# A hybrid decoder layer: x loaded features first, its norm factor applied in ACT's evacuations, the sample tile reordered, and a buffer of its own for the closing down-projection weights

## What is computed

```python
hn = rmsnorm(x, norm1_g)                   # x * rsqrt(mean(x*x) + eps) * g
proj = hn @ w_in                           # 1024 -> 3608 columns
# ... two head groups: gated linear attention (GLA), gated delta rule (GDN) with a short conv
x = x + mix @ w_out                        # 1024 -> 1024
hn2 = rmsnorm(x, norm2_g)
up = causal_dwconv(hn2 @ w_up, ...)        # 1024 -> 2 * 2816, width 3
x = x + (silu(a_f) * b_f) @ w_down         # 2816 -> 1024
y = rmsnorm(x, norm_f_g)
```

## Time and profile before

| what | value |
|---|---|
| median of three runs (lowest, highest) | 3583.7 us (3581.7, 3585.63) |
| the profiled execution's own time | 3583.03 us |
| its span, first to last instruction | 3581.2 us |
| mean granted TensorE clock | 0.984 |
| PE busy | 3482.3 us, 97% of the span |
| DVE, ACT, POOL busy | 58%, 24%, 16% |
| DMA | 225 MB, 63 GB/s over the span |
| mixer, start to barrier | 0 to about 1865 us |
| pass 0 and pass 1 of the MLP | from about 1866 us and from about 2683 us |

### The profile page before, as it was taken

One profiled execution on the slowest core, in us unless ns is written; L12 is line 12 of the kernel. 1 busy time (PEld: TensorE's weight loads), 2 busy tenths in 40 slices (PEclk: granted clock), 3 DMA queues, 4 the chain that ended last, 5 costly groups with the idle time before them and its releaser, 6 DMA issues. The chain is left out here.

```text
span 3581.2 us, 48600 instructions
## 1 busy us (share of the span) xinstructions
PE 3482.3 (97%) x16521; PEld 2439.3 (68%) x16521; DVE 2086.7 (58%) x4762; ACT 873.4 (24%) x1864; POOL 587.8 (16%) x921
## 2 busy tenths in 40 slices
PE   7999999999999999999789999999999999999997
PEld 4666666666666666666557777777758788778774
DVE  2456555545656554456335666656686666666666
ACT  2222322222233223222202212121223222222223
POOL 1111001111111011111143111111133211211110
PEclk9999999999999999999879999999999999999998
DMA  5022212111221211122541111111133111111101
GB/s 203 10 62 70 70 59 70 51 49 53 70 70 59 70 58 48 47 65 65 163 129 53 47 48 40 42 35 59 36 90 134 45 36 36 47 47 36 44 27 71
DMA packets 207293, 225.00 MB, mean 63 GB/s; under 512 B 12908, under 2 KB 151700, under 8 KB 207203
## 3 DMA queue, kind: packets, MB, share of 16 engines
q1 hardware_dynamic: 207203, 223.90, 20.2%
HBM read 194.19 MB, written 29.67 MB: 63 GB/s over the span
## 5 line engine op out<-in xcount | busy, mean ns | idle before, releaser
L613 PE MATMUL mixer_bank<-arena,hnt 128*128 128x451 f32 x2176 | 920.2, 552 | 2.2 <-DVE hnt L1213 1.5
L1837 PE MATMUL mlp_bank<-arena,ws 128*128 128x176 f32 (+1 forms) x3520 | 658.1, 340 | 10.9 <-ACT raw L2017 7.5
L1837 PEld LDWEIGHTS mlp_bank<-arena,ws 128*128 128x128 f32 x3520 | 589.4, 191 | 49.0 <-ACT raw L2017 9.2
L613 PEld LDWEIGHTS mixer_bank<-arena,hnt 128*128 128x128 f32 x2176 | 387.6, 191 | 296.4 <-issue 289.2
L1909 PE MATMUL mlp_bank<-arena 128*128 128x512 f32 x1120 | 493.7, 592 | 0.0
L2279 DVE TENSOR_TENSOR acc<-acc,mlp_bank 128x512 f32<-128x512 f32 x560 | 370.6, 685 | 57.1 <-PE mlp_bank L1909 54.5
L1909 PEld LDWEIGHTS mlp_bank<-arena 128*128 128x128 f32 x1120 | 211.5, 190 | 231.3 <-issue 205.7
L550 POOL TENSOR_TENSOR ex<-dtt,level 128x512 f32<-128x512 f32 (+1 forms) x114 | 143.1, 1255 | 1089.9 <-DVE dtt L1435 727.2
L2246 DVE SCALAR_TENSOR_TENSOR mcv<-raw,cf,mcv 128x512 f32<-128x512 f32 (+2 forms) x440 | 286.2, 667 | 60.9 <-ACT mcv L1990 50.5
L629 PE MATMUL mixer_bank<-wo,th 128*128 128x512 f32 (+1 forms) x544 | 265.5, 613 | 4.4 <-DMA wo<-in_w_out_dram 4.4
L1837 PE MATMUL mlp_bank<-arena 128*128 128x176 f32 (+1 forms) x1320 | 254.3, 343 | 10.9 <-POOL ident_mlp L2153 10.1
(11 more groups left out here) (323 smaller groups left out, 4176.2 us busy)
## 6 DMA issues: line engine op xcount, KB each, us to landing
wo<-in_w_out_dram SPq DMA_DIRECT2D x272, 256.0 KB, 2.8
arena<-in_w_up_dram SPq DMA_DIRECT2D x44, 512.0 KB, 5.1
wu<-in_w_up_dram SPq DMA_DIRECT2D x44, 512.0 KB, 5.1
arena<-in_w_down_dram SPq DMA_DIRECT2D x44, 512.0 KB, 4.2
arena<-in_w_in_dram SPq DMA_DIRECT2D x8, 1804.0 KB, 17.0
xt<-in_x_prompt_dram SPq DMA_DIRECT2D x16, 512.0 KB, 3.5
xr<-in_x_prompt_dram SPq DMA_DIRECT2D x16, 512.0 KB, 3.6
resid<-yo SPq DMA_DIRECT2D x16, 512.0 KB, 3.4
```

The costliest lines, as they stand in the source:

```text
L613: x = pe.matmul(bank[ring(g)][0:N, 0:GW], hnt[:, k, 0:N], w[:, k, g * GW:(g + 1) * GW], start=(k == 0), stop=(k == KT - 1))
L1837: x = pe.matmul(out[:, 0:N], left[:, k, :], xb[:, slot, k, g * N:(g + 1) * N], start=first and k == 0, stop=k == HK - 1, skip_group_check= ...
```

## The change

x is also given to the kernel features first, as `x_t`. The front of a tile loads both: `xt` for the sum of squares only, and `xc` (new, 128 x 8 x 128) with features on partitions. DVE multiplies `xc` by the gain straight into `hnt`; the multiplication by the factor and the eight turns are gone, and the factor is applied by ACT as the scale of its eight evacuations per tile, now ACTIVATE with a scale for each partition. Since `x_rs` must live until those are done, its last step moves behind the eighth.

In the sample tile the tanh and the norm sums use `th_s`, which lies in `xc`; DVE's second evacuation of the output projection stands behind the first predicated copies; all state loads stand behind the last slice of `w_out`; `keep_y` and the wait for the states stand behind the masked copies of q; the masked copies of k are made by ACT in place of POOL.

In the MLP the closing weights go into `wd_last`, which lies in the up-weights' buffer `wu[1]` and is loaded when the last up-product of the pass is done; loads at the boundary are reordered around it, and POOL makes only the first group of input sums at once and the others when the combinations are through.

```diff
+        xc = sb("xc", [C, KT, C])
+        th_s = xc[:, :, :].rearrange("p k i -> p (k i)")[:, 0:CT * S].rearrange("p (c i) -> p c i", c=CT)
...
         def _(sp):
+            x_columns = x_t.rearrange("(k p) n -> p k n", p=C)
+            sp.dma_start(xc[:, :, :], x_columns[:, :, 0:C]).then_inc(s_xc_loaded, 16)
             sp.dma_start(xt[:, :], x_prompt[0:C, :]).then_inc(s_x_loaded, 16)
...
             with sp.Fori(1, TILES - 2) as t:
                 before = sp.snap(t - 1)
-                sp.wait_ge(s_hn_turned, t + 2)
-                sp.dma_start(xt[:, :], x_prompt[bass.ds(t * C + 2 * C, C), :]).then_inc(s_x_loaded, 16)
+                rows = bass.ds(t * C + 2 * C, C)
+                sp.wait_ge(s_x_squared, t + 2)
+                sp.dma_start(xt[:, :], x_prompt[rows, :]).then_inc(s_x_loaded, 16)
+                sp.wait_ge(s_hn_out, t + 2)
+                sp.sem_inc(s_held, 1)
+                sp.dma_start(xc[:, :, :], x_columns[:, :, rows]).then_inc(s_xc_loaded, 16)
...
             for i in range(4, 20):
-                if i == 8:
-                    sp.wait_ge(s_hs_cleared, 1)
-                if 8 <= i < 12:
-                    sp.dma_start(hs_gla[rows_of[i - 8], i - 8, :, :], state_gla[i - 8]).then_inc(s_st_loaded, 16)
                 sp.wait_ge(s_wo_used, 16 * (t - 1) + i - 3)
                 wo_chunk(t - 1, i)
+            sp.wait_ge(s_hs_cleared, 1)
+            for h in range(H):
+                sp.dma_start(hs_gla[rows_of[h], h, :, :], state_gla[h]).then_inc(s_st_loaded, 16)
...
# gpsimd: the two loops of masked copies of k (L564 to L574) go; before the early input sums:
+            gp.wait_ge(s_masked_w, 1)
...
# tensor: front_turn is gone everywhere; the sample's norm sums read th_s
...
# scalar, evacuate
                 act.wait_ge(s_proj_done, GROUPS * (m - 1) + g + 1)
-                act.copy(proj[0:N, g * GW:(g + 1) * GW], bank[ring(g)][0:N, 0:GW]).then_inc(s_proj_out, 1)
+                act.wait_ge(s_x_rsed, m)
+                act.activation(proj[0:N, g * GW:(g + 1) * GW], bank[ring(g)][0:N, 0:GW], ACT.Identity,
+                               scale=x_rs[0:N, :]).then_inc(s_proj_out, 1)
...
# scalar, mixer
-                if out:
+                if out and not sample:
                     act.wait_ge(s_wo_used, 16 * t)
-                act.activation(th[:, :, 0:N], cv[:, :, 0:N], ACT.Tanh, scale=0.5).then_inc(s_conv_tanh, 1)
+                tq = th_s if sample else th
+                act.activation(tq[:, :, 0:N], cv[:, :, 0:N], ACT.Tanh, scale=0.5).then_inc(s_conv_tanh, 1)
...
                 fill(2)
+                if sample:
+                    act.wait_ge(s_proj_done, GROUPS * n)
+                    act.wait_ge(s_ked_out, n)
+                    for b in range(NB):
+                        x = act.activation(mk_gla[b], ked[0:S, :], ACT.Identity, scale=rows_s[:, b:b + 1])
+                    x.then_inc(s_masked_k, 1)
+                    act.wait_ge(s_kh_made, n)
+                    act.wait_ge(s_conv_stored, 16 * (NB + 1))
+                    for b in range(NB):
+                        x = act.activation(mk_gdn[b], kh[0:S, :, :], ACT.Identity, scale=rows_s[:, b:b + 1])
+                    x.then_inc(s_masked_k, 1)
...
                 inverse_rms(1, None)
                 fill(7)
+                front(2)
...
# vector
-            def front_norm(m, N):
-                dve.wait_ge(s_x_rsed, m)
-                dve.tensor_scalar(xt[0:N, :], xt[0:N, :], x_rs[0:N, :], None, ALU.mult)\
-                    .then_inc(s_x_normed, 1)
             def front_out(m, N):
-                dve.wait_ge(s_hn_turned, m)
+                dve.wait_ge(s_xc_loaded, 16 * m)
                 dve.wait_ge(s_proj_done, GROUPS * (m - 1))
-                for b in range(2):
-                    x = dve.tensor_tensor(hnt[:, 4 * b:4 * b + 4, 0:N], heads(b)[:, :, 0:N],
-                                          g1[:, 4 * b:4 * b + 4].unsqueeze(2).to_broadcast([C, 4, N]), ALU.mult)
-                x.then_inc(s_hn_out, 1)
+                dve.tensor_tensor(hnt[:, :, 0:N], xc[:, :, 0:N], g1[:, :].unsqueeze(2).to_broadcast([C, KT, N]),
+                                  ALU.mult).then_inc(s_hn_out, 1)
...
-                turn_levels(0 if sample else 6, NL + 1)
+                if sample:
+                    turn_levels(0, len(levels))
+                    evacuate_out(t, 1, C)
+                turn_levels(len(levels) if sample else 6, NL + 1)
...
                 if sample:
-                    dve.wait_ge(s_st_loaded, 16 * 2 * H)
                     dve.wait_ge(s_qg_made, n)
...
                     x.then_inc(s_masked_qk, 1)
+                    keep_y(t, C)
...
# mlp
+        wd_last = [wu[1][:, i, :, :].rearrange("p k n -> p (k n)") for i in range(2)]
...
             def loop(ps):
...
-                down(ps, PAIRS - 1)
+                if ps == 0:
+                    up(1, 0, 0)
+                sp.wait_ge(s_m3, group(ps, FT, 0))
+                for p in range(2):
+                    r0 = (2 * PAIRS - 2 + p) * C
+                    sp.dma_start(wd_last[p], w_down[r0:r0 + C, :]).then_inc(s_last_loaded, 16)
+
+            def scale(ps):
+                sp.wait_ge(s_down_done, first_out(ps, PAIRS - 1))
                 sp.dma_start(gf, norm_f_g.partition_broadcast(C).rearrange("p (e d) -> p e d", e=2))\
...
             loop(0)
-            up(1, 0, 0)
             x_blocks(1)
+            scale(0)
+            sp.wait_ge(s_down_done, Q0[1])
             up(1, 1, 1)
...
             loop(1)
+            scale(1)
...
             def close(ps):
-                pe.wait_ge(s_wd_loaded, 32 * PAIRS * (ps + 1))
+                pe.wait_ge(s_last_loaded, 32 * (ps + 1))
...
             def x_sums(ps):
+                gp.wait_ge(s_act_made, J0[ps])
                 for g in range(G):
+                    if g == 1:
+                        gp.wait_ge(s_combined, 21 * ps)
```

More of the change, by code:

```diff
@@ L405, in _ @@
                 wo_chunk(0, i)
[L406 to L409, removed]
+            for m in (2, 3):
+                rows = slice(m * C - C, m * C)
+                sp.wait_ge(s_x_squared, m - 1)
+                sp.dma_start(xt[:, :], x_prompt[rows, :]).then_inc(s_x_loaded, 16)
+                sp.wait_ge(s_hn_out, m - 1)
+                sp.dma_start(xc[:, :, :], x_columns[:, :, rows]).then_inc(s_xc_loaded, 16)
             with sp.Fori(1, TILES - 2) as t:
                 before = sp.snap(t - 1)
-                sp.wait_ge(s_hn_turned, t + 2)
-                sp.dma_start(xt[:, :], x_prompt[bass.ds(t * C + 2 * C, C), :]).then_inc(s_x_loaded, 16)
+                rows = bass.ds(t * C + 2 * C, C)
+                sp.wait_ge(s_x_squared, t + 2)
+                sp.dma_start(xt[:, :], x_prompt[rows, :]).then_inc(s_x_loaded, 16)
+                sp.wait_ge(s_hn_out, t + 2)
+                sp.sem_inc(s_held, 1)
+                sp.dma_start(xc[:, :, :], x_columns[:, :, rows]).then_inc(s_xc_loaded, 16)
                 wo_chunks(before, 20)
@@ L587, in _ @@
         def _(pe):
[L588 to L595, removed]
             def project(m, part, N):
@@ L985, in front_norm @@
                     act.wait_ge(s_x_lned, m)
+                    act.wait_ge(s_proj_out, GROUPS * (m - 1))
                     act.activation(x_rs[0:N, :], x_ln[0:N, :], ACT.Exp, scale=-0.5).then_inc(s_x_rsed, 1)
@@ L1097, in mixer @@
                 for p in range(2):
-                    x = act.activation(th[:, 4 * p:4 * p + 4, 0:N], heads(3 + p)[:, :, 0:N], ACT.Ln,
+                    x = act.activation(tq[:, 4 * p:4 * p + 4, 0:N], heads(3 + p)[:, :, 0:N], ACT.Ln,
                                        bias=eps4[:, :])
@@ L1103, in mixer @@
                 act.wait_ge(s_norm_ln, n)
-                act.activation(th[:, 0:4, 0:N], th[:, 0:4, 0:N], ACT.Exp, scale=-0.5, bias=lnq[:, :])
-                act.activation(th[:, 4:8, 0:N], th[:, 4:8, 0:N], ACT.Exp, scale=-0.5)\
+                act.activation(tq[:, 0:4, 0:N], tq[:, 0:4, 0:N], ACT.Exp, scale=-0.5, bias=lnq[:, :])
+                act.activation(tq[:, 4:8, 0:N], tq[:, 4:8, 0:N], ACT.Exp, scale=-0.5)\
                     .then_inc(s_norm_rs, 1)
@@ L1440, in mixer @@
                     .then_inc(s_ab_made, 1)
-                if out and sample:
-                    keep_y(t, C)
                 dve.wait_ge(s_egrow_made, n)
@@ L1912, in down, with plain @@
                         bank_free(ps, i, 28 + e)
-                        plain(bank[4 + e], 2 * p, 8, e, S)
-            def plain(out, a, t, e, N):
+                        plain(bank[4 + e], 2 * p, wd, 8, e, S)
+            def plain(out, a, right, t, e, N):
                 for j in range(2):
-                    x = pe.matmul(out[0:N, :], act_[a + j][:, t * C:t * C + N], wd[j][:, e * 512:e * 512 + 512],
+                    x = pe.matmul(out[0:N, :], act_[a + j][:, t * C:t * C + N], right[j][:, e * 512:e * 512 + 512],
                                   start=(j == 0), stop=(j == 1))
@@ L2411 @@
```

(3 more changed lines are left out.)

68 lines of the change are left out of this document (26 added, 42 removed).

## The result

The changed kernel takes 3552.2 us (median of four runs, 3550.79 to 3554.07) against 3584.28 for the kernel before, measured beside it; the ratio is 0.9914, with a 95% interval of 0.9902 to 0.9926. The forecast was 3550.5. The medians lie 32.1 us apart, where 32.5 were forecast. The profiled execution has a span of 3550.5 us, 30.7 less than before, and a granted clock of 0.988 instead of 0.984. PE's busy time fell by 28.0 us, to 3454.3, and ACT's rose to 25% of the span.

A forecast was written before the change was run, and what follows sets the result against it. PE, busy 99.7 of 100 us in the loop, was taken as the bound, with gains where it stands still: -3.4 + 0 - 9.5 - 12 - 7.6 = -32.5, taking 3583.03 to 3550.5 us; range 3539 to 3563.

The forecast's parts named there:

- The loop: Fifteen loop tiles: a wait for ACT's copy replaces the eight removed turns; change 0, ends +1 and -15.4 us.
- rival (a): Loop: the removed turns are worth their time, 15 x 1.03 us more gain, 3535 us; chance 0.06.
- Rival (b): Loop: the clock falls at the new wait, 1.7 us lost per tile, 26 in all, 3576 us; chance 0.08.
- Rival (c): Loop: the clock falls and stays low, 6.9 us per tile, 103 in all, 3653 us, slower; chance 0.04.
- The start: Ahead of tile 0's turns: ACT's copies begin 4.6 us earlier, less the new load; -3.4 us (-4.6 to -1.6).
- the 1.2 us taken off for the new load: Start: the 512 KB xc load costs 1.9 us less 0.7 of slack; bounds nothing and 3 us.
- The sample tile: Sample tile: L747 starts at 1764.3 instead of 1774.2, 9.9 us less; taken as -9.5, bounds 11.4 and 5.
- three edits act in series: Sample tile: GLA loads behind slices, tanh waiting only for taps, keep_y behind masked copies; then states are late; 9.5 us.
- The pass boundary: Between MLP passes: earlier closing-weight load removes a 5.11 us stall and close ends at 2671; -12 us (-5 to -13).
- they can cost a us that the earlier start of ACT there gives back: Pass 1, first groups: deferred input sums lie beside them, costing a us that ACT's earlier start offsets.
- Rival (d): Pass boundary: POOL and DVE still collide, half the gain there, 3556 us; chance 0.14.
- The end: Last close: the 5.98 us stall and the low clock behind it both go; -7.6 us, bounds -5 and -9.

## Why the prediction was right

**The loop** was the main decision, and it came out as argued: not the 15 x 1.03 of rival (a), but a wait of 0.87 in the place of turns of 1.03, the tile at 103.65 us as before (stretch +0.10). ACT's scaled evacuations took 0.64 us each where the copies took 0.53, the 0.1 that I gave them, and in the loop no wait of PE names them. Rival (b) did not come at 0.87 between the wide turns of the loop, but its mechanism is there: at 1.84 it takes 18 us, and ahead of the sample tile's narrow turns 0.87 is enough (with 0.17 in its place the clock stayed at 1.00). Rival (c), I wrote, decides from 2.2 us per tile on; the longer wait cost 2.2 per tile on average, wait and clock together, and just that brought the kernel level with the one before. A fall that stays for 14 us was not seen in the loop.

**The start** gave 5.03 where I had 3.4, and more than its bound of 4.6. The mis-sized step is the 1.2 us taken off for the new load. Its price was right (1.8 for another one; the 2304 KB of its working should be 2316, which changes nothing), and the 0.4 less for rows of 512 bytes, which rests on no number given there, did not show: another such load cost the full 1.8. The first product is 0.97 later:

```profile
12.17 7.78 PE L604 MATMUL mixer_bank<-arena,hnt 128*128 128x451 f32 x16 [12.17 <-DMA arena<-in_w_in_dram]
20.77 6.30 PE L604 MATMUL mixer_bank<-arena,hnt 128*128 128x451 f32 x16 [0.82 <-ACT proj L979]
```

But the first sixteen products took 9.09 and 7.78 here, where the next sixteen take 6.30, and the second group begins 0.2 earlier than before (21.00). The first products run at half the pace of the later ones. In the trace of the changed kernel the first four start 0.75 us or more apart and from the fifth on they start 0.38 apart; in the kernel before it is the first eight that start so far apart. That is half the pace, as at the lower level of the clock, although the column of the granted clock stands at 1.00 there. Two stretches of the changed kernel, then of the one with all sums at once, in the columns of the earlier trace rows; PE's count is the first in brackets:

```profile
13.00:15.00 2.00, 2.00 (x4) 1.01 (x3) 0.00 (x0) 0.20 (x1) 0.22 (x1) 1.00 0.65 153
15.00:17.00 2.00, 2.00 (x6) 0.95 (x5) 0.00 (x0) 0.00 (x0) 0.00 (x0) 1.00 1.00 347
```
```profile
15.00:17.00 2.00, 2.00 (x4) 0.89 (x3) 0.00 (x0) 0.00 (x0) 0.00 (x0) 1.00 1.00 332
17.00:19.00 2.00, 2.00 (x6) 1.02 (x6) 0.00 (x0) 0.00 (x0) 0.00 (x0) 1.00 1.03 381
```

In the kernels run here the first sixteen took 7.7 to 9.0, so how many run at half pace changes with no edit near them, and the part of the start's gain that came from it is luck. It is not the only one. The second tile's turns lie between 167.5 and 169.1 in the nine whose start is the changed kernel's (3.4 would have been 170.2), but not in the order of their first products. Where POOL makes the masked copies the second group begins at 21.83 and the turns come at 167.59, 0.9 before the changed kernel's, as the low clock behind tile 0's wait of 5.8 us ends sooner there (0.91 against 0.72 from 87 to 99 us). Sixteen small products there, then in the changed kernel:

```profile
89.22 1.11 PE L706 MATMUL mixer_bank<-qe,ex 64*128 64x64 f32 x16
```
```profile
88.20 1.97 PE L696 MATMUL mixer_bank<-qe,ex 64*128 64x64 f32 x16
```

ACT's first copies came 4.9 earlier (66.78 for 71.71), 4.7 if the 0.2 of the second group is taken off; I had 4.6.

**The sample tile**, -9.5 forecast, gave 9.51 from its first turns to the MLP's first product: 6.83 to L699 (6.7 forecast), 1.73 more to `gla_out`, and 0.95 behind, which I had at 0. That the two agree is in part luck: up to `gla_out`, which the 9.5 stood for, 8.56 were won where 9.9 had been worked out. It came 37.21 us after the tile's first turns, and 35.9 was worked out (1764.3 less 1728.43); 1760.7 looks like 1764.3 less the 3.4 of the start only because the start gave 5.0. My "three edits act in series" was right, but the experiments weigh them: the order of `keep_y` alone decides 8.6, the tanh 1.7, where the GLA states are loaded 0.2, and who makes the masked copies nothing.

**The pass boundary**, forecast -12, gave 11.58 up to pass 1, and then 3.17 were lost in pass 1. The step that failed is "they can cost a us that the earlier start of ACT there gives back": the deferred input sums hold POOL until 2668.75, its weight sums for the first pair come behind them, and these now fall on DVE's taps, whose inputs lie in SBUF too; PE waits, and its clock falls for the next products. So a collision moved, one step further than I looked. Of the 8.4 that remain, the load is 7.6 and the deferral 0.8 (6.4 won in close, 5.6 given back), which is less than the scatter of that stretch: whether the deferral is worth anything is not shown. Rival (d) had this mechanism in close; it came in pass 1.

**The end** gave 7.48 for 7.6. The two misses, 1.6 too little at the start and 3.6 too much at the boundary and in pass 1, partly cancel, so that 3550.5 lies nearer to 3552.2 than its terms deserve.

## What to carry to other kernels

Before you count the time of work that you remove, look at what ends next behind it on the other engines: if a latency is as long as the work, the gain is nothing until other independent work is put over it, and which wait stands ahead of which instruction is then the cheap thing to change (one moved wait: 11 us by the medians, 12 by the spans). Of several edits that act in series, find the one wait that they all end in, and ask of each semaphore whether its waiter needs all that it counts. A transfer or a sum that is deferred collides with what runs at the new place, and so does what is queued behind it; price that too.

## What was not expected of the hardware

A single wait of 1.84 us per tile on an otherwise busy PE set the clock to its lower level in 7 of 15 tiles and left it alone in 8, with the same instructions around it, and cost up to 3.3 us on top; at 0.87 us it never did in the fifteen waits of the loop, but did behind the sample tile's, where the turns are 32 wide. So the price of a stall is not linear: 0.97 us more of waiting came to 2.2 us per tile. At the start of the program the column of the granted clock says 1.00 while the products run at half pace; the spacing of like instructions is the better witness there.

POOL's tensor operations slowed DVE's combinations by a factor of 2.7 (three in 5.12 for 1.88), more than the time that POOL itself lost (2.0 to 2.1 for 1.68 each). Beside one long operation of DVE it was the other way round: in pass 1 of the changed kernel POOL's sum at 2659.92 took 2.69 us, and DVE's operation of 1024 columns at 2659.80 its usual 1.28.
